# Spatial gating inside the key selection's stage, ties in four passes, setup and first norm as one stage, and a ratio with two pointer scalars

## The chip, the core and the metric

The kernel runs on one core of a Trainium2 chip. The metric is the device time of one execution in microseconds. TensorE (PE), VectorE (DVE), ScalarE (ACT), GpSimd (POOL) and the DMA queues of SyncE (SP) and ScalarE each work through a list of their own, and meet at semaphores.

## The reference

One sequence of 1024 tokens of width 1024 goes through two layers of a first kind and then two of a second kind. The parts that matter here:

```python
def rms_norm(x, g):
    y = xf * lax.rsqrt(jnp.mean(xf * xf, axis=-1, keepdims=True) + EPS)
    return (y * g.astype(jnp.float32)).astype(x.dtype)
...
def diff_attention(q, k, v, lam, rel_bias):
        ...
        a = p[0] - lam * p[1]
...
def spatial_gating_unit(u, v, g_v, b_v, w_s, b_s):
    vn = layer_norm(v, g_v, b_v).reshape(bn, s // CHUNK, CHUNK, A_GROUPS, A_GDIM)
    w_m = jnp.where(causal[None], w_s, jnp.zeros_like(w_s))
    mixed = jnp.einsum('gts,bcsgd->bctgd', w_m, vn) + b_s.T[:, :, None]
    return u * mixed.reshape(bn, s, A_WIDTH_2)
...
        score = jnp.where(causal[None], score, -jnp.inf)
        _, idx = lax.top_k(score, top)          # top = 256 keys for each query
...
    y_a = jax.nn.silu(z_a) * spatial_gating_unit(u, v, v_norm_g, v_norm_b, w_spatial, b_spatial)
```

Besides these the kernel needs tables at its start: the cosines and sines of the positions, the bias of each relative position (`onehot` times `rel_bias`), the silu of the condition, and the scalar `lam` of each first-kind layer.

## The kernel before

The program is a row of stages (`Phase`). Each stage gives every engine one list, and between two stages all engines meet at a barrier, so a stage lasts as long as its slowest engine, and nothing of the next stage starts before, its loads included. Activations lie in SBUF as 8 tiles of 128 tokens or 8 tiles of 128 features. For exactness a float32 matrix product is made as three products of rounded halves (`hh`, `hl` of the activations, `w_hi`, `w_lo` of the weights). `ps` is PSUM, 8 banks of 128x512.

**Start.** `setup_phase` makes the tables. PE multiplies `relb` by `onehot` into four banks, DVE copies them to `rows`, and SP stores these and waits for the store. Behind its copies DVE reduces the angles for the sine. `norm_phase` then loads `x` (8 tiles of 512 KB), ACT sums the squares of each tile, POOL takes the power -0.5 of four tiles at a time, DVE scales the four, PE transposes them into one of four banks (16 units, u = half of the tokens and feature tile), ACT applies the gain into `n_full`, and DVE makes `hh` by a copy and `hl` by a subtraction. ACT waits until `hl` of the unit two before is made. The first projection follows (`w_hi` by ACT, `w_lo` by DVE, products at L695).

**End of the selection.** In each second-kind layer `select_project_phase` makes the last four groups of 512 columns of the input projection: the queries, two gates, and `u`, over 32 chunks of weights. For each chunk ACT makes `w_hi`, POOL `w_lo` (L2248), PE 24 products. In the same stage the keys are selected: for query blocks 2 to 7 a binary search over 32 bits finds the score of the 256th key. DVE counts for blocks 7, 3, 4 and 2 (`BY_DVE`), ACT for 5 and 6 (`BY_ACT`). Blocks are of 128 queries on the partitions, block qb has (qb + 1) * 128 keys. POOL meanwhile turns the queries and applies the gates (`apply_gate`, two operations for each of 16 units, L2242 and L2244, counted by `gated`). When the cuts stand, DVE counts the keys above each cut (L2138) and settles ties in five passes for each block:

```python
equal = (scores == cut)                       # L2202
rank = running sum of equal                   # L2203, tensor_tensor_scan
rank = (rank <= left over) * equal            # L2204
rank = (scores > cut) + rank                  # L2205
scores = (rank - 1) * 1e30                    # L2206, the mask added to the scores later
```

`u` is the last group that PE makes; ACT empties its 8 banks into `u_t` (L2073). Then `spatial_phase`, a stage of its own, loads the weights of the gating and their bias, POOL zeroes the upper triangle (L2452), PE mixes the tokens of each chunk into 8 banks (L2481), DVE adds the bias from PSUM and multiplies by `0.5 * u_t` into one of three `s_tmp` (L2467, L2471), and POOL multiplies `y` by it (L2457). After it come the sparse attention heads (`heads_phase`, tag `x_`).

**The ratio.** In the differential heads of the first kind DVE divides two row sums and multiplies by `neg_lam` (L1234, L1236); POOL scales a row of probabilities by it.

## Time and profile before

| | us |
|---|---|
| median of 3 runs | 3238.22 |
| lowest and highest | 3235.09 to 3243.04 |
| the profiled execution, by the same clock | 3231.08 |
| its span in the trace | 3229.4 |

The profile is that of one execution; its span runs from the first to the last recorded instruction, and 1.7 us lie around it. A row of the timeline gives the start in us from the span's start, the duration, the engine, the line of the kernel, the operation, and in brackets how long the engine had idled and what ended that. "x8" merges eight instructions that follow one another. The clock column is the share of TensorE's full clock that was granted.

### The profile page before, as it was taken

How to read it: one execution, taken by the hardware profiler on the slowest of the kernel's cores; microseconds unless marked ns; L12 is line 12 of the kernel's file. 1: busy time of each engine (PE TensorE's matmuls, PEld its weight loads, DVE VectorE, ACT ScalarE, POOL GpSimd, SP SyncE). 2: the span in 40 equal slices, each digit the busy share in tenths (PEclk: the TensorE clock that was granted, in tenths of full speed). 3: DMA queues.
4: the chain of work that ended last, by engine and by line, in shares of the span. 5: the costliest groups of instructions: out<-in, count | busy, mean ns of one | idle time of the engine just before them, and what ended most of it. 6: DMA issues, size and time to landing. Idle time of an engine off the chain costs nothing. (4 is left out here: it accounts for less than half of the span.)

```text
span 3229.4 us, 40985 instructions
## 1 busy us (share of the span) xinstructions
PE 2743.8 (85%) x13680; PEld 2185.2 (68%) x13680; DVE 2103.4 (65%) x4302; ACT 1588.9 (49%) x3077; POOL 1126.8 (35%) x965
## 2 busy tenths in 40 slices
PE   5999788798979997888989798994889698994887
PEld 3877566677868775667877575773767575773766
DVE  4472388688434624868865358887767358887866
ACT  3221276588422114758863226572864326572861
POOL 0010177455001003765530003972631003982631
PEclk9999899899989997999999899997989899997999
DMA  3343210100324321000022100110022100110022
GB/s 107 108 143 100 88 38 7 40 1 12 132 67 144 122 69 53 26 17 23 1 105 79 52 21 23 46 37 23 1 112 78 59 20 23 47 37 23 1 86 79
DMA packets 90752, 181.93 MB, mean 56 GB/s; under 512 B 12552, under 2 KB 27912, under 8 KB 90504
## 3 DMA queue, kind: packets, MB, share of 16 engines
q1 hardware_dynamic: 74124, 150.69, 14.4%
q10 hardware_dynamic: 16416, 28.61, 3.0%
q8 instruction: 109, 1.79, 0.2%
q14 instruction: 103, 0.84, 0.1%
HBM read 149.87 MB, written 33.33 MB: 57 GB/s over the span
## 5 line engine op out<-in xcount | busy, mean ns | idle before, releaser
L695 PE MATMUL ps<-w_hi,hh 128*128 128x512 f32 (+1 forms) x640 | 243.1, 380 | 24.1 <-DVE w_lo L580 12.0
L1277 POOL TENSOR_SCALAR a_prob<-a_prob,a_ratio 128x1024 f32<-128x1024 f32 x64 | 72.0, 1125 | 508.5 <-DVE a_ratio L1236 505.9
L695 PE MATMUL ps<-w_lo,hh 128*128 128x512 f32 (+1 forms) x640 | 240.4, 376 | 0.0
L1699 PE MATMUL ps<-o_w_hi,hh 128*128 128x512 f32 x512 | 212.8, 416 | 32.5 <-DVE o_w_lo L1623 32.5
L695 PE MATMUL ps<-w_hi,hl 128*128 128x512 f32 (+1 forms) x640 | 239.3, 374 | 0.0
L2138 DVE TENSOR_SCALAR_CACHE_REDUCE select_rows<-masks,select_cuts 128x640 bf16<-128x640 f32 (+7 forms) x268 | 233.3, 874 | 0.2
L1699 PE MATMUL ps<-o_w_lo,hh 128*128 128x512 f32 x512 | 206.7, 404 | 0.0
L1699 PE MATMUL ps<-o_w_hi,hl 128*128 128x512 f32 x512 | 206.3, 403 | 0.0
L974 POOL TENSOR_SCALAR b_prob<-b_prob,b_recip 128x1024 f32<-128x1024 f32 x128 | 144.3, 1127 | 170.5 <-DVE b_recip L939 168.0
L1679 POOL TENSOR_TENSOR o_rstd<-o_rstd,nhalf 128x1 f32<-128x1 f32 x56 | 46.7, 833 | 420.3 <-DVE o_rstd L1560 240.6
L1225 DVE CUSTOM_DVE_ANT_0 a_prob<-ps,a_bias 128x1024 f32<-128x1024 f32 x128 | 151.4, 1220 | 53.0 <-PE ps L1362 51.4
L916 DVE TENSOR_TENSOR b_attn_t_lo<-ps,b_attn_t_hi 128x512 fp32r<-128x512 f32 x256 | 163.7, 679 | 16.3 <-ACT b_attn_t_hi L850 15.9
L932 DVE TENSOR_REDUCE b_neg_max<-ps 128x1 f32<-128x1024 f32 x128 | 156.2, 1220 | 19.6 <-PE ps L1043 19.2
L1180 ACT ACTIVATE a_prob<-a_prob,a_neg_max 128x1024 f32<-128x1024 f32 x128 | 146.3, 1150 | 34.3 <-DVE a_neg_max L1225 34.3
L2282 PE MATMUL ps<-hh,w_hi 128*128 128x512 f32 x384 | 152.1, 396 | 8.1 <-ACT y L2073 5.4
L871 ACT ACTIVATE b_prob<-ps,b_neg_max 128x1024 f32<-128x1024 f32 x128 | 143.4, 1120 | 30.7 <-DVE b_neg_max L932 30.0
L695 PEld LDWEIGHTS ps<-w_hi,hh 128*128 128x128 f32 x640 | 121.5, 190 | 52.8 <-DVE w_lo L580 20.9
L1975 PE MATMUL ps<-w_hi,hh 128*128 128x512 f32 (+1 forms) x384 | 140.0, 365 | 17.6 <-DVE w_lo L1943 12.6
L850 ACT ACTIVATE b_attn_t_hi<-ps 128x512 fp32r<-128x512 f32 x256 | 139.7, 599 | 31.0 <-PE ps L1009 30.5
L1280 POOL TENSOR_TENSOR a_prob<-a_prob 128x1024 f32<-128x1024 f32 x64 | 152.6, 2385 | 5.3
L1362 PE MATMUL ps<-a_rows 64*128 64x512 f32 x768 | 119.4, 448 | 39.4 <-DVE a_neg_max L1225 35.8
L2282 PE MATMUL ps<-hh,w_lo 128*128 128x512 f32 x384 | 151.6, 395 | 0.0
(350 smaller groups left out, 8216.3 us busy)
## 6 DMA issues: line engine op xcount, KB each, us to landing
w_early<-in_w_in SPq DMA_DIRECT2D x108, 256.0 KB, 2.8
ada_w<-in_w_ada ACTq DMA_DIRECT2D x96, 256.0 KB, 2.7
w_raw<-in_w_in SPq DMA_DIRECT2D x84, 256.0 KB, 2.7
xcur<-aq SPq DMA_DIRECT2D x16, 512.0 KB, 3.8
y<-xcur SPq DMA_DIRECT2D x16, 512.0 KB, 4.1
a_bias<-bias_tiles SPq DMA_DIRECT2D x8, 960.0 KB, 4.8
bq<-in_w_out SPq DMA_DIRECT2D x12, 512.0 KB, 4.1
closing_rows<-in_w_out SPq DMA_DIRECT2D x12, 512.0 KB, 4.5
```

The source lines that it names most:

```text
L695: mm = nc.tensor.matmul(o, lhs, rhs, start=(k == 0 and i == 0), stop=(k == K - 1 and i == 2))
L871: nc.scalar.activation(prob(g), src, ACT.Exp, bias=nm[:, g % NS:g % NS + 1], scale=sign, accum_out=sums[:, g % NS:g % NS + 1]).then_inc(ex ...
L916: nc.vector.tensor_tensor(atl[:, kk % SLOTS, lo:], ps[:, bank(e), lo:], ath[:, kk % SLOTS, lo:].bitcast(F32), ALU.subtract).then_inc(tl_do ...
L932: nc.vector.tensor_reduce(out, ps[:, pair:pair + 2, :].rearrange("p b n -> p (b n)"), AX, ALU.max, negate=True).then_inc(shifted, 1)
L974: nc.gpsimd.tensor_scalar(prob(b), prob(b), rr[:, b % NS:b % NS + 1], 0.5, ALU.mult, ALU.mult).then_inc(normed, 1)
L1180: nc.scalar.activation(row, row, ACT.Exp, bias=nm[:, g % NS, m:m + 1], scale=-1.0, accum_out=out).then_inc(exped, 1)
L1225: nc.vector.tensor_tensor_reduce(out=row, in0=ps[:, 2 * m:2 * m + 2, :].rearrange("p b n -> p (b n)"), in1=bias, scale=-1.0, scalar=3.0e38 ...
L1280: nc.gpsimd.tensor_tensor(row0(g), row0(g), row1(g), ALU.add).then_inc(combined, 1)
L1699: mm = nc.tensor.matmul(o, lhs, rhs, start=(k == 0 and i == 0), stop=(k == K - 1 and i == 2))
L1975: mm = nc.tensor.matmul(ps[:, b, 0:n], lhs, rhs, start=(k == 0 and i == 0), stop=(k == K - 1 and i == 2))
L2138: spare_free[z] = mark(nc.vector.tensor_scalar(spare[:, z, 0:(qb + 1) * P], values, against, None, op, ALU.add, accum_out=column(count_of, ...
L2282: mm = nc.tensor.matmul(ps[:, b, :], lhs, rhs, start=(k == 0 and i == 0), stop=(k == K - 1 and i == 2))
```

## The change

There are four parts.

1. `opening_phase` takes the place of `setup_phase` and `norm_phase`. The loads of `x` stand first on SP's queue, then `onehot`, the gains and the tables, then the first two weight chunks. The positions stand first on ACT's queue. PE transposes first and multiplies `onehot` afterwards, into banks 4 to 7; their copies to `rows` go from DVE to ACT, behind its gains. ACT writes `hh` directly, rounded on writing, and DVE makes `hl` in one operation from PSUM; the `n_full` step is gone, and a bank is free when `hl` is made.
2. `spatial_phase` is gone. Its loads, its mask, its products and its additions stand in `select_project_phase`: the loads go into the weight buffers (`w_early` and `w_raw`) once all `w_lo` are made, PE mixes behind its last projection, POOL multiplies `y` by `u_t` ahead of the bias (`weigh_gate`) and by the biased mixture after (`mix`), and DVE writes that mixture over `u_t` (`add_bias`), two units behind each of the last four tie blocks. `mask_weights` is the mask of L2452. The factor 0.5 is applied where ACT empties `u`.
3. The ties take four passes, with `rank` in the buffer of the gates' tanh (so DVE first waits for all gates, `gated` at 32). Blocks 5 and 6 are counted by ACT, by one more sign pass each; DVE counts its own four before the wait.
4. The ratio is a `tensor_scalar` with two pointer scalars.

```diff
+                for t in range(T):
+                    sp.dma_start(xt[:, t, :], x_from[t * P:(t + 1) * P, :]).then_inc(x_in[t], 16)
                 sp.dma_start(onehot[:, :], a["onehot"]).then_inc(bias_in, 16)
                 sp.dma_start(relb[:, :], a["rel_bias"]).then_inc(bias_in, 16)
+                sp.dma_start(env["g_cols"][:, :, :], a["pre_norm_g"]).then_inc(kept_in, 16)
...
                         kept_in, 16)
+                for ch, (tile, sem) in enumerate(early.slots):
+                    sp.dma_start(tile, early.weights(ch)).then_inc(sem, 16)
                 sp.wait_ge(copied, 4)
                 sp.dma_start(env["bias_rows"].ap(), rows[:, :]).then_inc(stored, 16)
                 sp.wait_ge(stored, 16)
...
+                for t in range(Q):
+                    square(t)
                 act.wait_ge(cond_in, 16)
                 nc.scalar.activation(cth[:, :], cin[:, :], ACT.Tanh, scale=0.5).then_inc(bent, 1)
+                for t in range(Q, T):
+                    square(t)
                 act.wait_ge(dotted, 1)
                 nc.scalar.activation(dots[:, :, :], dots[:, :, :], ACT.Exp).then_inc(exped, 1)
                 for e in range(2):
                     act.wait_ge(reduced, e + 1)
                     nc.scalar.activation(trig[:, e, :, :], red[:, e, :, :], ACT.Sin).then_inc(waved, 1)
+                act.wait_ge(kept_in, 96)
+                for u in range(2 * K):
+                    h, k = divmod(u, K)
+                    act.wait_ge(turned, u + 1)
+                    nc.scalar.activation(hh[:, k, h * BANK:(h + 1) * BANK], ps[:, u % 4, :], ACT.Identity,
+                                         scale=gain_cols[:, k:k + 1]).then_inc(gained, 1)
+                for n in range(4):
+                    act.wait_ge(mult, n + 1)
+                    nc.scalar.activation(rows[:, n * BANK:(n + 1) * BANK], ps[0:A_HEADS, 4 + n, :],
+                                         ACT.Copy).then_inc(copied, 1)
 
...
+                pe.wait_ge(made, 2)
+                for u in range(2 * K):
+                    h, k = divmod(u, K)
+                    pe.wait_ge(rows_ready, (h + 1) * Q)
+                    if u >= 4:
+                        pe.wait_ge(lo_done, u - 3)
+                    for j in range(Q):
+                        mm = nc.tensor.transpose(ps[:, u % 4, j * P:(j + 1) * P],
+                                                 xt[:, h * Q + j, k * P:(k + 1) * P], ident[:, :])
+                    mm.then_inc(turned, 1)
                 pe.wait_ge(bias_in, 32)
                 for n in range(4):
-                    nc.tensor.matmul(ps[0:A_HEADS, n, :], relb[:, :], onehot[:, n * BANK:(n + 1) * BANK],
+                    nc.tensor.matmul(ps[0:A_HEADS, 4 + n, :], relb[:, :], onehot[:, n * BANK:(n + 1) * BANK],
                                      start=True, stop=True).then_inc(mult, 1)
...
+                def split(u):
+                    h, k = divmod(u, K)
+                    dst = slice(h * BANK, (h + 1) * BANK)
+                    dve.wait_ge(gained, u + 1)
+                    nc.vector.scalar_tensor_tensor(hl[:, k, dst], ps[:, u % 4, :], gain_cols[:, k:k + 1],
+                                                   hh[:, k, dst].bitcast(F32), ALU.mult, ALU.subtract).then_inc(lo_done, 1)
...
+                scale_rows(0)
+                dve.wait_ge(bent, 1)
+                step(nc.vector.tensor_scalar(cth[:, :], cth[:, :], 1.0, 0.5, ALU.add, ALU.mult))
+                nc.vector.tensor_tensor(env["cond"][:, :], cin[:, :], cth[:, :], ALU.mult)
+                scale_rows(1)
+                for u in range(2 * K):
+                    split(u)
...
-                    nc.vector.scalar_tensor_tensor(r, s0[:, g % NS0:g % NS0 + 1], neg_lam, r, ALU.mult,
-                                                   ALU.mult).then_inc(ratio_done, 1)
+                    nc.vector.tensor_scalar(r, s0[:, g % NS0:g % NS0 + 1], neg_lam, r, ALU.mult,
+                                            ALU.mult).then_inc(ratio_done, 1)
...
+        rank_row = th[:, :, :].rearrange("p e n -> p (e n)")
+        wt = early.tile[:, :, :].rearrange("p e (g t) -> p (e g) t", t=P)
+        bs = w_raw[:, 0, :].rearrange("p (g t) -> p g t", t=P)
...
                             sp.dma_start(gb[:, e * BANK:(e + 1) * BANK], row(a[name][l])).then_inc(rows_in, 16)
+                sp.wait_ge(lo_done, C)
+                sp.dma_start(wt, a["w_spatial_2"][l]).then_inc(spatial_w_in, 16)
+                for e in range(2):
+                    src = a["b_spatial_2"][l].rearrange("(p e) t -> e p t", e=2)[e].unsqueeze(0).broadcast_to(
+                        [HD, K // 2, P])
+                    sp.dma_start(bs[e * HD:(e + 1) * HD, :, :], src).then_inc(spatial_b_in, 16)
...
-                        nc.scalar.activation(dst, ps[:, b, :], ACT.Copy).then_inc(emptied, 1)
+                        nc.scalar.activation(dst, ps[:, b, :], ACT.Copy, scale=0.5 if g == U else 1.0).then_inc(emptied, 1)
...
+                for j, qb in enumerate(BY_ACT):
+                    act.wait_ge(moved, 2 * (2 * BITS - 1) + j + 1)
+                    nc.scalar.activation(verdict[:, j:j + 1], negcut[:, j:j + 1], ACT.Identity,
+                                         bias=env["nhalf"][:, 0:1]).then_inc(judged, 1)
+                for j, qb in enumerate(BY_ACT):
+                    n = (qb + 1) * P
+                    act.wait_ge(judged, 2 * 2 * BITS + j + 1)
+                    nc.scalar.activation(spare[:, 2 + j, 0:n], scores(qb), ACT.Sign, bias=verdict[:, j:j + 1],
+                                         accum_out=signs[:, j:j + 1]).then_inc(above, 1)
                 empty(U)
...
+                def add_bias(z):
+                    p, h = units[z]
+                    if z == 0:
+                        dve.wait_ge(spatial_b_in, 32)
+                    dve.wait_ge(mixed, z + 1)
+                    dve.wait_ge(weighed, z + 1)
+                    nc.vector.tensor_tensor(half_of(u_t, p, h).rearrange("p (c t) -> p c t", t=P),
+                                            ps[:, z, :].rearrange("p (c t) -> p c t", t=P),
+                                            bs[:, p, :].unsqueeze(1).broadcast_to([P, 4, P]), ALU.add).then_inc(biased, 1)
...
-                dve.wait_ge(moved, 4 * BITS)
-                last = mark(nc.vector.tensor_scalar(cut[:, 4:6], negcut[:, :], -1.0, None, ALU.mult))
-                after(last)
-                for qb in ORDER:
+                for qb in BY_DVE:
                     last = count(qb, column(cut, qb), scores(qb), ALU.is_gt)
                 after(last)
-                after(mark(nc.vector.tensor_scalar(count_of[:, :], count_of[:, :], -1.0, float(TOPK), ALU.mult, ALU.add)))
-                for qb in ORDER:
+                mark(nc.vector.tensor_scalar(count_of[:, 0:4], count_of[:, 0:4], -1.0, float(TOPK), ALU.mult, ALU.add))
+                last = mark(nc.vector.tensor_scalar(minus[:, 0:4], cut[:, 0:4], -1.0, None, ALU.mult))
+                after(last)
+                dve.wait_ge(gated, 4 * T)
+                for i, qb in enumerate(ORDER):
                     n = (qb + 1) * P
-                    equal, rank = work[:, 0, 0:n], work[:, 1, 0:n]
+                    equal, negative = work[:, 0, 0:n], column(minus, qb)
+                    rank = rank_row[:, 0:n]
+                    if qb in BY_ACT:
+                        j = BY_ACT.index(qb)
+                        negative = negcut[:, j:j + 1]
+                        dve.wait_ge(moved, 4 * BITS)
+                        dve.wait_ge(above, j + 1)
+                        mark(nc.vector.tensor_scalar(column(cut, qb), negative, -1.0, None, ALU.mult))
+                        after(mark(nc.vector.tensor_scalar(column(count_of, qb), signs[:, j:j + 1], -0.5, TOPK - 0.5 * n,
+                                                           ALU.mult, ALU.add)))
                     after(mark(nc.vector.tensor_scalar(equal, scores(qb), column(cut, qb), None, ALU.is_equal)))
                     after(mark(nc.vector.tensor_tensor_scan(rank, equal, equal, 0.0, ALU.add, ALU.bypass)))
-                    after(mark(nc.vector.scalar_tensor_tensor(rank, rank, column(count_of, qb), equal, ALU.is_le, ALU.mult)))
-                    after(mark(nc.vector.scalar_tensor_tensor(rank, scores(qb), column(cut, qb), rank, ALU.is_gt, ALU.add)))
-                    after(mark(nc.vector.tensor_scalar(scores(qb), rank, 1.0, -MASKED, ALU.subtract, ALU.mult)))
+                    after(mark(nc.vector.scalar_tensor_tensor(rank, rank, column(count_of, qb), scores(qb), ALU.is_gt,
+                                                              ALU.subtract)))
+                    mark(nc.vector.tensor_scalar(scores(qb), rank, negative, MASKED, ALU.is_gt, ALU.mult))
+                    if i >= 2:
+                        add_bias(2 * i - 4)
+                        add_bias(2 * i - 3)
...
+                    pool.wait_ge(emptied, 8 * U + z + 1)
+                    nc.gpsimd.tensor_tensor(half_of(y, p, h), half_of(y, p, h), half_of(u_t, p, h),
+                                            ALU.mult).then_inc(weighed, 1)
+
+                def mix(z):
+                    p, h = units[z]
+                    pool.wait_ge(biased, z + 1)
+                    nc.gpsimd.tensor_tensor(half_of(y, p, h), half_of(y, p, h), half_of(u_t, p, h),
+                                            ALU.mult).then_inc(y_done, 1)
 
                 for ch in range(C):
...
+                mask_weights()
+                pool.wait_ge(gated, 4 * T)
+                for z in range(8):
+                    weigh_gate(z)
+                for z in range(8):
+                    mix(z)
...
+                pe.wait_ge(masked, 1)
+                pe.wait_ge(v_ready, T)
+                for z, (p, h) in enumerate(units):
+                    pe.wait_ge(emptied, 8 * U + z + 1)
...
+                            mm = nc.tensor.matmul(ps[e * HD:(e + 1) * HD, z, c_ * P:(c_ + 1) * P],
+                                                  v[:, 4 * h + c_, feats], wt[:, 2 * p + e, :], start=True, stop=True)
+                    mm.then_inc(mixed, 1)
```

The removed functions are printed above, and `scale_rows` and `square` do what their loops in `norm_phase` did. The order in which the engines issue their work shows two places. ScalarE at the program's start, before the change (`n_sq` is the squares of `x`, `trig` the sines, the branches are the ends and starts of stages):

```order
L272 ACTIVATE c_tanh<-c_in 128x8
L274 ACTIVATE lam_dots<-lam_dots 128x4
L277 ACT_TABLE_LOAD
L277 ACTIVATE trig<-reduced 128x256 x2
L86 UNCONDITIONAL_BRANCH
L359 UNCONDITIONAL_BRANCH
L365 ACTIVATE n_sq,n_ss<-n_x 128x1024 x8
L372 ACTIVATE n_full<-ps,g_cols 128x512 x16
L86 UNCONDITIONAL_BRANCH
```

and after it:

```order
L284 ACTIVATE n_sq,n_ss<-n_x 128x1024 x4
L299 ACTIVATE c_tanh<-c_in 128x8
L284 ACTIVATE n_sq,n_ss<-n_x 128x1024 x4
L303 ACTIVATE lam_dots<-lam_dots 128x4
L306 ACT_TABLE_LOAD
L306 ACTIVATE trig<-reduced 128x256 x2
L311 ACTIVATE hh<-ps,g_cols 128x512 x16
L315 ACTIVATE rows<-ps 4x512 x4
L86 UNCONDITIONAL_BRANCH
```

The squares now stand ahead of the tanh and the sines, the 16 gains write `hh`, and the four copies of `rows` close the stage.

VectorE from the last count of the selection to the second tie block, before (the scan prints as SCALAR_TENSOR_TENSOR):

```order
L2198 TENSOR_SCALAR select_counts<-select_counts 128x6
L2202 TENSOR_SCALAR select_rows<-masks,select_cuts 128x1024
L2203 SCALAR_TENSOR_TENSOR select_rows<-select_rows 128x1024
L2204 SCALAR_TENSOR_TENSOR select_rows<-select_rows,select_counts 128x1024
L2205 SCALAR_TENSOR_TENSOR select_rows<-masks,select_cuts,select_rows 128x1024
L2206 TENSOR_SCALAR masks<-select_rows 128x1024
L2202 TENSOR_SCALAR select_rows<-masks,select_cuts 128x512
```

and after the change, the third and the fourth tie block, and the start of the fifth:

```order
L2234 TENSOR_SCALAR select_rows<-masks,select_cuts 128x640
L2235 SCALAR_TENSOR_TENSOR p_tanh<-select_rows 128x640
L2236 SCALAR_TENSOR_TENSOR p_tanh<-p_tanh,select_counts,masks 128x640
L2238 TENSOR_SCALAR masks<-p_tanh,select_minus 128x640
L2185 TENSOR_TENSOR u_t<-ps,w_raw 128x512 x2
L2234 TENSOR_SCALAR select_rows<-masks,select_cuts 128x384
L2235 SCALAR_TENSOR_TENSOR p_tanh<-select_rows 128x384
L2236 SCALAR_TENSOR_TENSOR p_tanh<-p_tanh,select_counts,masks 128x384
L2238 TENSOR_SCALAR masks<-p_tanh,select_minus 128x384
L2185 TENSOR_TENSOR u_t<-ps,w_raw 128x512 x2
L2231 TENSOR_SCALAR select_cuts<-select_negcuts 128x1
L2232 TENSOR_SCALAR select_counts<-select_signs 128x1
```

A block has four passes, `rank` lies in `p_tanh`, the additions of the bias (`u_t<-ps,w_raw`) come in pairs behind a block, and the two small operations at a block of ACT's turn its sums into a count.

## Rows read from the trace of the kernel before

**Rows 1.** The page, busy time of each engine over the span.

```profile
PE 2743.8 (85%) x13680; PEld 2185.2 (68%) x13680; DVE 2103.4 (65%) x4302; ACT 1588.9 (49%) x3077; POOL 1126.8 (35%) x965
```

**Rows 2.** Stretches: length, busy time of each engine, clock, DMA share, GB/s.

```profile
0.00:21.67 21.67, 6.98 (x8) 0.82 (x8) 10.03 (x30) 3.81 (x6) 1.00 (x9) 1.00 0.28 58
...
21.67:58.37 36.70, 13.01 (x65) 10.08 (x65) 23.12 (x44) 21.34 (x34) 2.04 (x2) 0.89 0.33 129
...
2171.82:2207.29 35.47, 11.09 (x48) 8.67 (x46) 34.34 (x44) 4.79 (x8) 1.02 (x1) 0.72 0.00 0
...
2207.29:2232.35 25.06, 9.08 (x128) 8.84 (x128) 14.20 (x16) 0.00 (x0) 11.23 (x9) 0.70 0.11 32
```

**Rows 3.** Timeline of the start: start us, us, engine, line, operation, [idle before].

```profile
4.65 6.98 PE L283 MATMUL ps<-onehot,relb 32*4 32x512 f32 x8 [4.65 <-DMA relb<-in_rel_bias]
...
12.37 0.33 SPq L246 DMA_DIRECT2D bias_rows<-rows  x1
...
13.67 1.28 ACT L277 ACT_TABLE_LOAD   x1
...
21.67 3.85 SPq L348 DMA_DIRECT2D n_x<-in_x  x8
...
25.30 1.06 ACT L365 ACTIVATE n_sq<-n_x 128x1024 f32<-128x1024 f32 x1 [5.78 <-DMA n_x<-in_x]
...
31.63 2.74 DVE L384 TENSOR_SCALAR n_x<-n_x,n_rstd 128x1024 f32<-128x1024 f32 x4 [1.14 <-POOL n_rstd L356]
...
55.51 0.42 DVE L390 CAST hh<-n_full 128x512 fp32r<-128x512 f32 x1
...
58.37 0.79 PE L695 MATMUL ps<-w_hi,hh 128*128 128x512 f32 x1 [6.69 <-DVE w_lo L580]
```

**Rows 4.** Two stretches of 1 us within the transposes, columns as in the second group.

```profile
44.00:45.00 1.00, 0.84 (x5) 0.47 (x4) 0.97 (x3) 0.62 (x2) 0.00 (x0) 0.50 0.00 0
...
48.00:49.00 1.00, 0.56 (x5) 0.36 (x5) 0.97 (x3) 0.69 (x1) 0.00 (x0) 1.00 0.00 0
```

**Rows 5.** One line: a split of a PSUM bank; ns min/median/max.

```profile
L1203 DVE SCALAR_TENSOR_TENSOR a_rows<-ps,a_rows x32: 673/690/693, 370.5 to 1368.1; 128x512 fp32r<-128x512 f32 x32
```

**Rows 6.** VectorE's timeline at the end of the selection and in the gating.

```profile
2162.93 0.33 DVE L2163 TENSOR_SCALAR select_cuts<-select_kept,select_cuts 128x1 f32<-128x1 f32 x2
...
2171.82 1.04 DVE L2193 TENSOR_SCALAR select_cuts<-select_negcuts 128x2 f32<-128x2 f32 x1 [8.55 <-ACT select_negcuts L2097]
...
2178.43 0.75 DVE L2202 TENSOR_SCALAR select_rows<-masks,select_cuts 128x1024 f32<-128x1024 f32 x1
...
2206.66 0.63 DVE L2206 TENSOR_SCALAR masks<-select_rows 128x896 f32<-128x896 f32 x1
...
2222.19 1.26 DVE L2471 SCALAR_TENSOR_TENSOR s_tmp<-s_tmp,u_t 128x512 f32<-128x512 f32 x1
```

**Rows 7.** GpSimd's and ScalarE's timelines in the same stretch.

```profile
2170.29 1.29 POOL L2244 TENSOR_TENSOR y<-y,p_tanh 128x512 f32<-128x512 f32 x1
...
2213.08 1.10 POOL L2452 TENSOR_SCALAR_AFFINE_SELECT s_wt<-s_wt 128x1024 f32<-128x1024 f32 x1 [40.24 <-DMA s_wt<-in_w_spatial]
...
2231.09 1.26 POOL L2457 TENSOR_TENSOR y<-y,s_tmp 128x512 f32<-128x512 f32 x1 [0.63 <-DVE s_tmp L2471]
...
2178.12 5.42 ACT L2073 ACTIVATE u_t<-ps 128x512 f32<-128x512 f32 x8 [6.40 <-PE ps L2282]
```

**Rows 8.** Groups by line on VectorE: busy us, mean ns.

```profile
L2205 DVE SCALAR_TENSOR_TENSOR select_rows<-masks,select_cuts,select_rows 128x1024 f32<-128x1024 f32 (+5 forms) x12 | 11.4, 952 | 0.4
```

**Rows 9.** VectorE's timeline beside a busy GpSimd, and that stretch.

```profile
1994.67 2.01 DVE L2148 TENSOR_TENSOR masks<-masks,select_rows 128x768 int32<-128x768 int32 x1
...
1997.38 1.09 DVE L2148 TENSOR_TENSOR masks<-masks,select_rows 128x896 int32<-128x896 int32 x1
...
1994.07:2009.23 15.16, 13.31 (x50) 10.74 (x51) 14.77 (x13) 10.30 (x29) 14.24 (x9) 0.82 0.39 104
```

**Rows 10.** One line: the ratio of the differential heads.

```profile
L1236 DVE SCALAR_TENSOR_TENSOR a_ratio<-a_sums,neg_lam,a_ratio x64: 218/220/1859, 385.4 to 1413.0; 128x1 f32<-128x1 f32 x64
```

227 lines of the change are left out of this document (68 added, 159 removed).

## The prediction

> **What bounds the kernel now.** I read the page first. TensorE is busy 85% of the span [rows 1], but that is an average, and a change inside one stage is worth what that stage's slowest engine gives. So I cut the trace at the barriers around the change [rows 2]. There TensorE is nearly idle. In the first stage it works 7.0 us of 21.7, in the next 13.0 of 36.7. From the moment the cuts stand in a second-kind layer (2171.8) to the last tie (2207.3) it works 11.1 of 35.5, VectorE 34.3. In the gating stage it works 9.1 of 25.1, VectorE 14.2 and GpSimd 11.2. These stretches are chains on VectorE and GpSimd that nothing covers. The second such layer lies 728 us later and I take it as the same, since it runs the same lists. The stretches come to 58.4 + 2 x 60.5 us, and the change touches all of them.
>
> **The start, now 58.4 us to the first projection product** [rows 3]. Today SP issues the loads of `x` at 21.7, behind the tables, and ACT squares the first tile at 25.3. Now they are issued at about 0.8. The first tile then lands at some 4.5 (3.6 after its issue, as today), ACT has issued its own loads and loaded its table (1.28) by 5.5. Four squares take until 30.3 today (the scaling at 31.63 less the 1.14 for the power and 0.17 for the variance), so 1.26 each. Eight, the tanh, and up to 1 us for table loads that share the queues (28% busy over the first 21.7 us, [rows 2]) end at 17.0. ACT then has the exponential, one more table load of 1.28 and two sines: gains can begin at 19.4. VectorE's table work of 7.3 us (its 10.0 busy in [rows 2] less four copies of 0.68) lies below the squares. Its second half waits for the squares: 17.0 + 0.17 + 1.14 + 2.74 = 21.1, and there the splits begin.
>
> Each split is one operation from PSUM, 0.69 [rows 5], or 0.61 to 0.66 from start to start; today a copy (0.42) and a subtraction (0.69) make 1.06 from start to start, and the last pair begins at 55.5 [rows 3]. Sixteen take 10.6: to 31.7, and VectorE's last table steps 1.3 more, 33.0. But a new tail is longer. TensorE gets its last transposes when split 12 of 16 is done (29.0), ends them at 29.8, and only then multiplies `onehot`. That took 6.98 us [rows 3] behind an idle engine, which I take for the low level of the clock. Inside the transposes of today the granted clock stands at the low level in one microsecond and at full in another [rows 4], so it is 3.5 or 7.0. Then come ACT's last copy (0.7), the store's issue (0.33, [rows 3]) and its landing. How long the store takes does not show; 3.6 is the first load's time to its use, and I take 2.2, with 1.5 to 3.6 as bounds. The stage ends between 36.5 and 40.5, I take 38.2. From VectorE's last subtraction to the first product today it is 1.7 (58.37 less 56.65, the end of the pair that began at 55.51). So the first product stands at about 39.9 where it stood at 58.4: **18.5 us less**, from 16.2 to 20.3 by these bounds. `w_early` is in by then. Moving the `rows` copies off VectorE costs nothing more than this tail, since ACT has nothing behind its gains.
>
> **The selection's tail, twice.** Today VectorE ends the search at 2163.3, waits 8.55 us for ACT's cuts, and has counted all blocks at 2178.4 [rows 6]. Now it counts its own four in that gap (3.3 us) and waits for the last gate, which GpSimd ends at 2171.6 [rows 7]. So ties begin at 2171.65: 6.8 less. ACT's two added sign passes (2.3 us) end at 2174.3; it next empties `u` at 2178.1 [rows 7], so they lie in its idle time, and without that cover they would delay TensorE's mixing by 2.3 only, which isn't late.
>
> Five passes over six blocks took 2178.4 to 2207.3, 28.9. The dropped one is 11.4 / 2 = 5.7 per layer [rows 8] and its gaps 0.2: 23.0 remain. Two pairs of small operations at ACT's blocks add 0.6, eight additions of the bias from PSUM 8 x 0.66 = 5.3. Alone, VectorE would end at 2171.65 + 28.9 = 2200.6.
>
> It isn't alone. GpSimd masks at about 2177 (the load waits for the last `w_lo` at 2172.8; from the load to the mask it was 4.2), multiplies from 2178.8 as the banks are emptied, and mixes behind the additions: 1.1 + 8 x 1.29 + 6 x 1.27 = 19.0 us of work before the last pair. Rows of today show what that costs. A 768-wide operation of VectorE with two SBUF inputs took 2.01 us, a 896-wide one 1.09 [rows 9]. Over that stretch of 15.16 GpSimd is busy 14.24; VectorE's twelve passes there would take 9.3 at the rate of the 1.09, so it loses 5.9 us to 12 or so of GpSimd's work, 0.5 per us. In the gating stage an operation of 0.69 takes 1.26 beside a GpSimd one [rows 6], 0.45 per us. The additions read PSUM and keep their time, so some 3 of the 19 us fall where they harm nothing. I take 0.58 per us, a little above both rows because the tie passes leave no gaps: 16 x 0.58 = 9.3, ties end at 2209.9. The last two mixes end 1.9 later, 2211.8. TensorE mixes at 2183 to 2192 (9.1 of work, [rows 2]) and isn't waited for.
>
> The stage and the gating together ended at 2232.35 [rows 7]: 20.6 less in each layer, **41 for both**. What becomes late next is GpSimd's last pair.
>
> The Trainium skill (GPSIMD Engine Reference, Key points) says that GpSimd shares its SBUF interfaces with VectorE and contends with operations in a two-port mode or with two SBUF inputs, which is what a tie block consists of; the rows above agree. It speaks against this part, and gives no price. A sum by it with every microsecond of GpSimd's work added to VectorE's (a loss of 1) is the second rival; with the rows' loss it is the sum above.
>
> **The ratio.** 64 operations of 0.22 us [rows 10]. The new form shows nowhere with two pointers; the nearest rows with one pointer are the search's steps at 0.15 to 0.2, so it gains at most 64 x 0.05 = 3 us, loses no more, and most lies beside other work. I take 0.
>
> **Sum.** 18.5 + 41 = 59.5 off the profiled execution's 3231.1 is 3171.6. The median of the runs is 7 us above that execution; off 3238.2 it is **3179**, the number I give, since what is measured is a median.
>
> **The rivals.**
>
> *Light contention.* GpSimd's work hardly slows the ties, as it doesn't slow the search's counts. Ties end at 2200.6, the stage at 2202.6: 29.8 per layer, and with the start's 18.5 some 78, so 3160. For it: some passes may use one input only. Against: both rows of [rows 9]. 10%.
>
> *Full serialisation.* Each microsecond of GpSimd is lost to VectorE: ties end at 2200.6 + 16, the stage at 2218.5, 13.8 per layer: 46 in all, 3192. For it: GpSimd's eight multiplies stand back to back, as in no stretch of the gating. 15%.
>
> *The start gives half.* The loads of `x` share the queues with small pieces: over the first 21.7 us they are 28% busy with little data (58 GB/s), so 6.1 us of queue time. If all of it came first, squares, splits and the store all stand up to 6 us later, at the low clock and with the slow store 8: 10 in place of 18.5, 3187. 10%.
>
> *Slower.* GpSimd as the new bound: 16 operations from 2178.8. They decide from the point where they end past 2232.4, that is from 3.35 us each; alone they take 1.29 [rows 7]. At 4 us each the stage would end at 2243 and the kernel, both layers counted, 2 us slower, the start's gain included. Nothing in the rows comes near. 1%.
>
> *The change does nothing.* It would need the gain to be given back at a later DMA wait, of 60 us. The loads of the next stages are issued inside them, so they move along. 2%.
>
> The forecast has 62%. The range takes in light contention to full serialisation: 3160 to 3197, the upper end also for a store and clock at their slow bounds with it. A measurement of this kernel tells 0.3%, about 10 us, from no change. All cases but the last two lie 40 us and more below, so faster has 0.97, same 0.02, slower 0.01.
>
> **What the profile of the changed kernel would show.** The first projection product at 38 to 42 us; splits at a spacing of 0.61 to 0.7 from about 21; the `onehot` products behind the transposes, with VectorE idle at the stage's end. The first tie pass 0.1 us behind the last gate, some 8.3 us behind the search's last step. Tie passes of 128x1024 and of 128x512 at today's times before GpSimd's multiplies begin and longer under them, additions of the bias still 0.68. From the last gate to the barrier some 40 us, 61 today. It is wrong if that stretch is nearer 31 or 47, or if the transposes begin past 20 us, which would mean that the loads of `x` came late.

## The result

The changed kernel takes 3182.94 us, the median of 4 runs (3181.74 to 3185.18), the kernel before 3239.69 (3235.09 to 3243.04, 4 runs). The ratio is 0.9826, 95% interval 0.9813 to 0.984: faster by 52 to 61 us. The forecast was 3179, with a range of 3160 to 3197.

The page and three stretches of the changed kernel, columns as in [rows 1] and [rows 2]:

```profile
PE 2747.1 (86%) x13680; PEld 2191.3 (69%) x13680; DVE 2070.8 (65%) x4254; ACT 1594.8 (50%) x3093; POOL 1154.7 (36%) x981
...
0.00:20.00 20.00, 0.34 (x2) 0.36 (x3) 9.17 (x26) 11.18 (x20) 2.08 (x11) 1.00 0.90 258
...
2155.92:2198.69 42.77, 18.44 (x177) 15.80 (x175) 40.00 (x36) 7.21 (x15) 26.93 (x18) 0.77 0.07 19
2163.18:2176.93 13.75, 11.18 (x146) 9.91 (x144) 13.54 (x11) 4.08 (x7) 13.75 (x9) 1.00 0.01 1
```

The second stretch runs from the last gate to the barrier and takes 42.77 us, where it was 2232.35 - 2171.58 = 60.77 [rows 7]. VectorE is busy in 40.0 of it: it is still the chain. The third is GpSimd's eight first multiplies. Both engines are full there, and more than half of the loss turned out to lie there (6.7 of 11.0 us, run 6).

The timeline of the start, columns as in [rows 3]:

```profile
0.79 4.04 SPq L244 DMA_DIRECT2D n_x<-in_x  x8
...
5.07 1.06 ACT L284 ACTIVATE n_sq<-n_x 128x1024 f32<-128x1024 f32 x1
...
8.21 11.02 SPq L251 DMA_DIRECT2D b_ada_cols<-in_b_ada_cols  x1
...
18.23 1.06 ACT L284 ACTIVATE n_sq<-n_x 128x1024 f32<-128x1024 f32 x1 [0.91 <-DMA n_x<-in_x]
...
23.45 2.42 ACT L311 ACTIVATE hh<-ps,g_cols 128x512 fp32r<-128x512 f32 x4 [1.94 <-DMA qk_gain<-in_k_norm_g]
24.18 11.26 DVE L353 SCALAR_TENSOR_TENSOR hl<-ps,g_cols,hh 128x512 fp32r<-128x512 f32 x16 [0.42 <-ACT hh L311]
...
33.51 3.59 PE L332 MATMUL ps<-onehot,relb 32*4 32x512 f32 x8
...
37.75 0.32 SPq L259 DMA_DIRECT2D bias_rows<-rows  x1
...
41.95 0.79 PE L681 MATMUL ps<-w_hi,hh 128*128 128x512 f32 x1 [4.86 <-DVE w_lo L566]
```

The first product stands at 41.95 us where it stood at 58.37 [rows 3]. Read from the top: the loads of `x` are issued at once, but the squares of tiles 2 to 8 each wait 0.4 to 0.9 us for their load and end at 19.3 in place of the forecast 17.0. The splits begin at 24.2 (forecast 21.1), and the stage ends with the chain named in the prediction: last transposes, `onehot` products, a copy, a store.

The selection's end in the first such layer, VectorE's ties and GpSimd's part:

```profile
2156.02 1.70 DVE L2234 TENSOR_SCALAR select_rows<-masks,select_cuts 128x1024 f32<-128x1024 f32 x1 [4.01 <-POOL y L2279]
...
2163.30 2.26 DVE L2235 TENSOR_TENSOR_SCAN p_tanh<-select_rows 128x512 f32<-128x512 f32 x1
...
2168.55 1.56 DVE L2234 TENSOR_SCALAR select_rows<-masks,select_cuts 128x640 f32<-128x640 f32 x1
2170.14 2.44 DVE L2235 TENSOR_TENSOR_SCAN p_tanh<-select_rows 128x640 f32<-128x640 f32 x1
...
2190.66 2.96 DVE L2235 TENSOR_TENSOR_SCAN p_tanh<-select_rows 128x896 f32<-128x896 f32 x1
...
2195.45 1.28 DVE L2185 TENSOR_TENSOR u_t<-ps,w_raw 128x512 f32<-128x512 f32 x2
```

```profile
2163.18 13.75 POOL L2289 TENSOR_TENSOR y<-y,u_t 128x512 f32<-128x512 f32 x8 [0.86 <-ACT u_t L2077]
...
2196.21 2.48 POOL L2295 TENSOR_TENSOR y<-y,u_t 128x512 f32<-128x512 f32 x2 [4.47 <-DVE u_t L2185]
```

The first tie follows the last gate by 0.1 us, as forecast. The scan of 512 columns takes 2.26 us beside GpSimd, the additions from PSUM keep their 0.64 each. One sign of the prediction failed: the first pass, of 1024 columns, was to keep its 0.75 us and takes 1.70, beside GpSimd's last `w_lo` (2155.87 to 2157.17).

### The profile page after: what moved, and what is told of

Same layout as the page of the kernel before. It is cut to its first block and busy times, and to the rows that moved or that the text cites. A ratio compares the mean times of both kernels' runs of the same rounds, so it can differ in the third digit from the quotient of the medians.

```text
span 3183.4 us, 40934 instructions
## 1 busy us (share of the span) xinstructions
PE 2747.1 (86%) x13680; PEld 2191.3 (69%) x13680; DVE 2070.8 (65%) x4254; ACT 1594.8 (50%) x3093; POOL 1154.7 (36%) x981
## 5 line engine op out<-in xcount | busy, mean ns | idle before, releaser
L2151 DVE TENSOR_SCALAR_CACHE_REDUCE select_rows<-masks,select_cuts 128x1024 bf16<-128x1024 int16 (+7 forms) x264 | 229.7, 873 | 0.2
L918 DVE TENSOR_REDUCE b_neg_max<-ps 128x1 f32<-128x1024 f32 x128 | 156.2, 1221 | 20.1 <-PE ps L1029 19.7
L502 ACT ACTIVATE w_hi<-w_raw 128x512 fp32r<-128x512 f32 (+1 forms) x56 | 33.7, 601 | 239.4 <-PE ps L681 229.7
```

Source lines behind the costliest of these rows:

```text
L918: nc.vector.tensor_reduce(out, ps[:, pair:pair + 2, :].rearrange("p b n -> p (b n)"), AX, ALU.max, negate=True).then_inc(shifted, 1)
L2151: spare_free[z] = mark(nc.vector.tensor_scalar(spare[:, z, 0:(qb + 1) * P], values, against, None, op, ALU.add, accum_out=column(count_of, ...
```

## The experiments

All times below are medians; the ratio stands against runs of the kernel before on the same chip, taken beside them. Before took 3234.18 us beside runs 1 to 4, 3229.87 beside runs 5 to 7 (one execution each), 3237.83 beside runs 8 to 11 and 3236.09 beside run 12. The code shown with a run is shortened to what matters.

**1. The opening alone.** The kernel before with the change's `opening_phase` only.

```diff
+opening_phase(... x_from, gain_cols, hh, hl ...)   # as changed
 select_project_phase, spatial_phase, the ratio       # as before
```

> The kernel before with the opening stage alone (selection, ties, gating and ratio as before). If the parts are independent, the gain is what stands between the two traces at the first projection product, 58.37 against 41.95: 16.4 us, so 3223, and that product at 42. The rival, that the opening's gain is partly given back at a later wait (the two traces differ by 46 us at the end where 16.4 + 2 x 18 = 52.4 were gained in the changed stages), gives 10 us, 3230.

3221.68 us, ratio 0.9955 (0.9939 to 0.9971): 14.6 us less, 9 to 20 by the interval. The first product stands at 41.53, so the stage alone gives the 16.8 us of the trace. Whether later stages give some of it back isn't told: the interval holds both the 16.4 and the rival's 10.

**2. The selection's stage alone**, with the opening and the ratio of before.

```diff
+select_project_phase   # as changed, gating inside
-spatial_phase
 opening_phase, the ratio   # as before
```

> The kernel before with the selection, the ties and the gating of the change (opening and ratio as before). Independent parts: 60.8 us from the last gate to the barrier become 42.8 in each layer, 36 us less, 3204. The rival, that the stages behind give some of it back because TensorE has idled since 2182 and comes cold (6 us missing between the traces), gives 30, 3210.

3206.16 us, ratio 0.9897 (0.9872 to 0.9922), 25 to 41 us less: its runs scatter (3196.61 to 3212.53), so it doesn't tell the two apart. The traces say a little more: the heads' stage behind the selection takes 157.1 and 158.2 us here, 157.5 and 155.9 in the kernel before, so that stage gave back 1.9 of the 6 in this pair. With the first run the two parts sum to 48 us; the whole gave 52 to 61. The parts add up within what the runs tell.

**3. Five passes in place of four**, all else as changed.

```diff
-rank = (rank > count) - scores;  scores = (rank > -cut) * MASKED
+rank = (rank <= count) * equal;  rank = (scores > cut) + rank
+scores = (rank - 1) * -MASKED
```

> The changed kernel with five passes for each tie block, as before, all else as changed. If GpSimd's work costs VectorE a fixed sum (so many us lost for each us of its work), the fifth pass adds what it costs alone, 5.7 + 0.2 in each layer: 12 us, 3195. The rival, that passes are stretched by a factor all through (40.7 us where 28.9 would do, 1.4), gives 8.3 in each layer, 16.6 us, 3199.5. In the trace: from the last gate to the barrier 48.7 or 51.1.

3191.77 us, ratio 0.9863 (0.9847 to 0.9879), some 12 us above the changed kernel (0.0037 of 3238). The stage's end is where ScalarE begins the next one:

```profile
2204.22 1.06 ACT L820 ACTIVATE x_stage<-kv 128x1024 fp32r<-128x1024 f32 x1 [37.52 <-PEq L86]
```

In the changed kernel that row stands at 2199.02; from the first tie it is 49.35 us here and 43.00 there. The dropped pass was worth some 6.3 us a layer, near its own length (5.7, [rows 8]) and not the rival's 8.3: GpSimd's work is a fixed amount, and with it the loss, so one more pass stretches into the time when GpSimd is idle.

**4. The bias by TensorE.** A product with one row of weights puts the bias into PSUM ahead of each of the 64 value products; VectorE's addition becomes the multiplication by the gate, and GpSimd's mixes go.

```diff
+matmul(o, ones[1 row], brow[p], start=True, stop=False)
-matmul(o, v, wt, start=True, stop=True)
+matmul(o, v, wt, start=False, stop=True)
-u_t = ps + bs        (VectorE);  y = y * u_t   (GpSimd)
+y = ps * y           (VectorE)
```

> The changed kernel with the bias of the gating added by TensorE (one product of a row of ones and the bias ahead of each product), so that VectorE multiplies PSUM by y into y in place of adding the bias, and GpSimd's eight second multiplies fall away. The contention theory: six of them lie beside the tie passes and cost 6 x 1.29 x 0.6 = 4.6, the last two end 2.0 behind VectorE: 6.6 us less in each layer, 13 in all, 3170. If only the tail counts (the contention comes from the first eight alone), 4 in all, 3179. The added products take TensorE some 14 us in each layer where it idles; if they come too late for the multiplies, VectorE waits and the gain is gone.

3273.96 us, ratio 1.0118 (1.0101 to 1.0134), slower than before. VectorE's timeline, and TensorE's:

```profile
2196.32 0.69 DVE L2182 TENSOR_TENSOR y<-ps,y 128x512 f32<-128x512 f32 x1 [6.74 <-PE ps L2346]
```

```profile
2181.41 0.68 PE L2345 MATMUL ps<-w_raw,ones 1*64 1x128 f32 x2
2182.02 0.69 PE L2346 MATMUL ps<-w_early,v 128*64 128x128 f32 x2
...
2180.00:2190.00 10.00, 10.00 (x34) 4.58 (x32) 3.02 (x5) 0.00 (x0) 0.00 (x0) 0.50 0.00 0
```

Each product, of either kind, takes 0.62 us from start to start, and a unit 9.87. VectorE waits for seven of the eight units: TensorE needs 75.7 us for all (2169.93 to 2245.6), where the expectation had 14 for the added products. The clock stands at its low level, 0.50, in this stretch; ahead of it, at 1.00, a product takes 0.36 (2170 to 2174). The low clock alone isn't it, as run 8 shows.

**5. GpSimd idle behind the mask.** `y` leaves out both multiplications of the gating.

```diff
-dve.wait_ge(weighed, z + 1)       # in add_bias
-for z in range(8): weigh_gate(z)
-for z in range(8): mix(z)
```

> The changed kernel without GpSimd's sixteen multiplies of the gating in each second-kind layer, so y there is the gate alone; GpSimd still masks the weights. If GpSimd's work is all that stretches the ties, VectorE needs what it needs alone: 28.9 us from the last gate to its last addition, plus 0.7 beside the last w_lo and 0.6 beside the mask, so 30 where it took 40.8, and the barrier comes 2.0 earlier still. The rival, that the new forms of the passes (pointer scalars, rank in another buffer) are slower by themselves, leaves 35 or more.

One execution, 3158.01 us. Ties begin at 2155.92 and the last addition ends at 2185.67: 29.75 us.

```profile
2155.92 1.70 DVE L2233 TENSOR_SCALAR select_rows<-masks,select_cuts 128x1024 f32<-128x1024 f32 x1 [4.02 <-POOL y L2278]
...
2161.97 1.32 DVE L2233 TENSOR_SCALAR select_rows<-masks,select_cuts 128x512 f32<-128x512 f32 x1
2163.33 1.23 DVE L2234 TENSOR_TENSOR_SCAN p_tanh<-select_rows 128x512 f32<-128x512 f32 x1
...
2165.78 0.55 DVE L2233 TENSOR_SCALAR select_rows<-masks,select_cuts 128x640 f32<-128x640 f32 x1
2166.36 1.49 DVE L2234 TENSOR_TENSOR_SCAN p_tanh<-select_rows 128x640 f32<-128x640 f32 x1
...
2180.54 2.02 DVE L2234 TENSOR_TENSOR_SCAN p_tanh<-select_rows 128x896 f32<-128x896 f32 x1
```

Every pass that lay beside a multiplication is back at its own time: 1.23 for 2.26, 0.55 for 1.56, 1.49 for 2.44, 2.02 for 2.96. The first pass (1.70) still lies beside the last `w_lo`, and one of 512 columns (1.32) beside the mask. So the multiplications cost 40.8 - 29.75 = 11.0 us per layer, and the last mixes add 2.0 behind. The rival, new forms that are slower by themselves (35 or more), fell.

**6. Mixes without weighs.** The gating leaves out the factor `u`; the eight mixes stay.

```diff
-dve.wait_ge(weighed, z + 1)       # in add_bias
-for z in range(8): weigh_gate(z)
```

> The changed kernel without GpSimd's first eight multiplies (y times u), so the gating leaves out u. Ten us of work less beside the ties. At a loss of 0.65 per us VectorE ends 6.7 earlier, 34 us from the last gate to its last addition; if work on both sides is serialised (loss 1), 10 earlier, 30.5.

One execution, 3170.26 us. The ties begin at 2158.53 and the last addition ends at 2192.59, 34.06 us. So the six mixes beside the ties cost VectorE 4.3 us and the eight weighs the other 6.7. At the 1.27 and 1.29 us that one takes alone [rows 7] that is 0.56 and 0.65 us per us of GpSimd's work, or 0.7 and 0.8 us for each multiplication. A loss of 1 per us (30.5) fell.

**7. The loads of `x` with less beside them.** ScalarE's small loads go to SP's queue behind the eight loads of `x`.

```diff
 sp.dma_start(xt[t], x[t])   # x8
+sp.dma_start(cin, ...); sp.dma_start(lam_in, ...); sp.dma_start(consts, ...); sp.dma_start(g_in, ...)
-act.dma_start(cin, ...)   # and the other three
-scale_rows(0)    # VectorE: behind the lambda steps
+scale_rows(0)    # VectorE: ahead of them
```

> The changed kernel with ACT's queue issuing only the two loads for the angles at the start; the condition, lam, constants and g_sub loads go to SP's queue behind x, and VectorE does the lam steps behind the first scaling. The eight squares run from 5.07 to 19.4 now, 1.8 a piece. If the loads on ACT's queue slow those of x, the pace goes back to the 1.26 of before, the squares end at 15, and all stands some 3 us earlier (the first projection product at 39). The rival, that the queues are slow in the first microseconds whatever is issued, or that x is slowed by what stands behind it on its own queue, leaves the squares' end at 19 and the product at 42.

One execution, 3185.71 us, first product at 42.02: nothing gained.

```profile
10.19 1.06 ACT L291 ACTIVATE n_sq<-n_x 128x1024 f32<-128x1024 f32 x1
...
15.83 0.21 ACT L299 ACTIVATE c_tanh<-c_in 128x8 f32<-128x8 f32 x1 [4.49 <-DMA c_in<-in_c]
```

The fourth square ends at 11.3 where it ended at 11.8; then ScalarE waits 4.49 us for `c_in`, which now stands behind `x`. From there on the squares find their tiles landed and end at 20.1. The edit brought its own wait, so it doesn't tell how much the small loads cost `x`; that stays open.

**8. The bias by TensorE in one batch.** Sixteen bias products of 512 columns ahead of all 64 value products; the rest as in run 4.

```diff
+for e in range(2):
+    for z in range(8): matmul(ps[e, z, :], ones[1 row], brow[p] x4, start=True, stop=False)
 for z in range(8): for c_, e: matmul(ps[...], v, wt, start=False, ...)
```

> The changed kernel with the spatial bias put into PSUM by TensorE, in 16 products of 512 columns and one row of weights that all stand ahead of the 64 value products, so that the two kinds do not alternate; VectorE then multiplies PSUM by the gate in place of adding the bias, and GpSimd's eight mixes go. If alternation was what made the earlier form cost 9.9 us a unit, the last add ends where it did in the run whose GpSimd work stopped after the mixes' place, with the eight weighs alone charged: 34 us from the first tie becomes about 36.5 (29.75 plus 0.6 of 11 to 14 us of weighs less what they no longer meet), and the 2.0 us of the last mix go: 4 to 6.5 us per layer, 3170 to 3175 us in all. If the cost sits in the value products themselves once a group of accumulation is open, the units still take over 5 us each and the kernel is slower than the changed one, 3210 us or more.

3198.95 us, ratio 0.988 (0.9866 to 0.9893): by the ratios 77 us faster than run 4, 17 slower than the changed kernel. TensorE's groups here (busy us, mean ns), and three stretches:

```profile
L2343 PE MATMUL ps<-w_raw,ones 1*64 1x512 f32 x32 | 19.7, 906 | 0.0
L2351 PE MATMUL ps<-w_early,v 128*64 128x128 f32 x128 | 9.8, 331 | 0.0
...
2166.80:2169.00 2.20, 2.20 (x7) 0.71 (x7) 2.18 (x2) 0.60 (x1) 2.20 (x2) 1.00 0.00 0
...
2172.00:2186.00 14.00, 14.00 (x21) 3.56 (x19) 3.27 (x3) 0.00 (x0) 4.46 (x3) 0.50 0.00 1
...
2186.40:2190.00 3.60, 3.60 (x35) 3.60 (x36) 0.69 (x1) 0.00 (x0) 0.00 (x0) 0.50 0.00 0
```

A product has two records. In the last row, with the clock at 0.50, 35 records take 3.60 us, 0.10 each; in run 4, at the same 0.50, 34 take 10.0, 0.29 each. So a value product took 0.62 us when one-row products stood between, and 0.21 in a row of its kind: alternation cost it 0.4 us. The Trainium skill (TensorEngine Tiling (Array Packing), Key Properties) says that a change of the tiling mode drains TensorE. The trace agrees that the change is what costs; that one row of weights is such a mode, no run here shows. My second expectation there, over 5 us a unit in the value products, fell (1.2). But the first did too, since it had no time for the bias products: sixteen of 512 columns take 19.7 us, during which the clock falls from 1.00 to 0.50 (at the pace of the first stretch, 7 records in 2.20 us, they would take 10, an estimate), and VectorE waits for them:

```profile
2188.42 0.69 DVE L2182 TENSOR_TENSOR y<-ps,y 128x512 f32<-128x512 f32 x1 [13.08 <-PE ps L2351]
```

**9. The bias rows early.** The four `onehot` products go between transposes, the copies between gains, and the gains wait for `g_cols` alone.

```diff
 for u in range(16): transposes(u)
+    if u in (4, 6, 8, 10): onehot product (u - 4) / 2
 for u in range(16): gain(u)
+    if u in (6, 8, 10, 12): copy of row (u - 6) / 2
```

> The changed kernel with the four bias rows' products and copies interleaved with the middle of the opening's transposes instead of standing behind them, and with the norm's gain columns waited for by themselves. The theory that the opening ends with the chain of last transposes, 3.6 us of products, a copy and a store of 2.3 us behind them expects the stage to end with VectorE's tables at about 37 us in place of 40.2, the first product of the next stage at about 38.7 in place of 41.95, and 3.2 us less, 3180. The rival, that the copies placed inside the loop slow a ScalarE that is as busy there as VectorE (0.69 us against 0.70 per unit), gives back up to 4 x 0.59 = 2.4 us of it, 3182.

3188.18 us, ratio 0.985 (0.9836 to 0.9864): 5 us slower than the changed kernel by the medians, 8 by the ratios, against both expectations. TensorE's groups in 24 to 44 us, here and then in the changed kernel:

```profile
L330 PE MATMUL ps<-ident,n_x 128*128 128x128 f32 x48 | 10.7, 403 | 1.3 <-DVE hl L359 1.3
L338 PE MATMUL ps<-onehot,relb 32*4 32x512 f32 x8 | 7.5, 1034 | 0.0
```

```profile
L327 PE MATMUL ps<-ident,n_x 128*128 128x128 f32 x48 | 8.2, 325 | 2.0 <-DVE hl L353 1.9
L332 PE MATMUL ps<-onehot,relb 32*4 32x512 f32 x8 | 3.6, 587 | 0.0
```

The same records take longer: 403 ns against 325, 1034 against 587. That is TensorE's low clock. Duration of one transpose (ns, min/median/max) in the kernel before, at a granted clock of 0.50 and of 1.00 [rows 4], then here, then in the changed kernel:

```profile
L403 PE MATMUL ps<-ident,n_x x12: 336/418/448, 43.7 to 46.8; 128*128 128x128 f32 x12
L403 PE MATMUL ps<-ident,n_x x9: 272/273/301, 47.9 to 50.0; 128*128 128x128 f32 x9
```

```profile
L330 PE MATMUL ps<-ident,n_x x8: 421/421/475, 38.4 to 40.0; 128*128 128x128 f32 x8
L330 PE MATMUL ps<-ident,n_x x7: 272/273/273, 41.3 to 41.9; 128*128 128x128 f32 x7
```

```profile
L327 PE MATMUL ps<-ident,n_x x9: 421/421/421, 26.4 to 28.1; 128*128 128x128 f32 x9
L327 PE MATMUL ps<-ident,n_x x14: 272/273/300, 28.8 to 31.0; 128*128 128x128 f32 x14
```

The clock rose at 41 us here, after a stretch in which a `onehot` product stood behind every eight transposes, and at 28 us in the changed kernel, after transposes alone. Run 11, with the same order, shows 41.7. How the small products hold it down isn't shown. The clock column doesn't show this. It reads 1.00 wherever the trace has no clock entry, and the first entries stand at 41.2 and 28.5 us; the 1.00 in the first stretch of [rows 2] is no measurement either.

TensorE is busy without a gap from 26 to 42 us, gains and splits wait for its transposes, the last split ends at 44.3 in place of 35.4, and the next stage's first product stands at 47.2. The bound moved to TensorE, which neither of my theories had named.

**10. The ratio's old instruction** in the changed kernel.

```diff
-tensor_scalar(r, s0, neg_lam, r, mult, mult)
+scalar_tensor_tensor(r, s0, neg_lam, r, mult, mult)
```

> The changed kernel with the ratio's instruction of before (218 to 220 ns each in the trace of before, against 273 ns for the form with two pointer scalars). The theory that VectorE is not what ends these stages expects no change against the changed kernel, 3183 us plus or minus 3. The rival, that 64 instructions longer by 53 ns lie on the path in part, expects 1.5 to 3.5 us less, 3180 or under.

3182.91 us, ratio 0.9827 (0.9813 to 0.9841): no difference, though an interval of 4.5 us to each side can't exclude the rival's 1.5 to 3.5. The traces do: from the first product to the end of the span it is 3141.3 us here and 3141.5 in the changed kernel. The instruction itself differs, changed kernel first, then this one:

```profile
L1222 DVE TENSOR_SCALAR a_ratio<-a_sums,neg_lam,a_ratio x64: 271/273/276, 369.6 to 1395.0; 128x1 f32<-128x1 f32 x64
```

```profile
L1222 DVE SCALAR_TENSOR_TENSOR a_ratio<-a_sums,neg_lam,a_ratio x64: 219/220/1875, 367.3 to 1398.1; 128x1 f32<-128x1 f32 x64
```

The new form is 53 ns longer, 3.4 us of VectorE over 64 of them, and none of it shows.

**11. Runs 8, 9 and 10 together.**

> The batched bias, the early bias rows and the ratio's old instruction together in the changed kernel. If each gives what it is expected to give alone (8 to 13 us, 3.2 us, 0 us), 3167 to 3172 us.

3202.71 us, ratio 0.9892 (0.9878 to 0.9905), some 21 us above the changed kernel. The losses of 8 (17) and 9 (8) add up nearly; nothing new.

**12. The gating's multiplications by VectorE.** GpSimd does none; VectorE weighs, adds and mixes between the ties.

```diff
-for z in range(8): weigh_gate(z)   # GpSimd
-for z in range(8): mix(z)          # GpSimd
+for work in (weigh, add_bias, mix): work(2 * i - 4); work(2 * i - 3)   # VectorE
```

> The changed kernel with the eight weighs and eight mixes of the spatial gate done by VectorE, between the ties, in place of GpSimd; GpSimd is idle behind the mask. VectorE's part without any multiply took 29.75 us from first tie to last add; 16 multiplies of 128x512 from SBUF at 0.62 to 0.66 us (half of the 1.23 to 1.29 that two of them or one of 1024 columns take in the traces) add 10.1 to 10.6, so the last one ends 40.1 us behind the first tie, and nothing follows it. The theory that GpSimd's multiplies cost VectorE 0.56 to 0.65 us per us (13.75 + 6 x 2.7 us of them, 11.0 us lost, and 2.0 us of tail) expects the stage to end 2.4 us sooner per layer than with GpSimd, 3178 us in all. The rival, that the loss is not contention but a wait for GpSimd's results that the ties absorb, expects VectorE to lose with each multiply that it takes over, and the stage to end no sooner, 3183 to 3190.

3174.9 us (3172.08 to 3177.68, 5 runs), ratio 0.981 (0.9785 to 0.9834): 8 us less than the changed kernel by the medians, 5 by the ratios, and the two intervals overlap. The times alone don't settle it; the trace does. VectorE's first tie and last mix, and the next stage's first row:

```profile
2158.68 1.70 DVE L2243 TENSOR_SCALAR select_rows<-masks,select_cuts 128x1024 f32<-128x1024 f32 x1 [4.01 <-POOL y L2289]
...
2196.83 1.29 DVE L2185 TENSOR_TENSOR y<-y,u_t 128x512 f32<-128x512 f32 x2
...
2198.41 1.06 ACT L820 ACTIVATE x_stage<-kv 128x1024 fp32r<-128x1024 f32 x1 [27.90 <-PEq L86]
```

From first tie to last mix it is 39.4 us (expected 40.1), and from first tie to the next stage 39.7, where the changed kernel takes 43.0: 3.3 us a layer. Doing one multiplication costs VectorE 0.6 us (39.4 - 29.75 for sixteen); one that GpSimd did beside it cost 0.8 (11.0 for fourteen). So VectorE gains 1.3 us, and the tail of 2.0 goes. The rival, that VectorE loses with each one it takes over, fell.

## Why the prediction held

**The selection's tail: right in its steps, short in the loss beside GpSimd.** Ties start at the last gate (0.1 behind it). ScalarE's added passes and TensorE's mixing were covered. From the last gate to the barrier it took 42.8 us where 40.2 was forecast. Of the 2.6, run 5 puts 0.85 in what is left without the multiplications (29.75, forecast 28.9), and 1.7 in the loss beside them (11.0, forecast 9.3). The 29.75 isn't VectorE alone, though. In it the first pass lies beside the last `w_lo` (1.70 for 0.75) and another beside the mask (1.32 for 0.48), 1.8 us together. Without these VectorE's own work is 28.0, 0.9 below the forecast, and GpSimd's work beside it cost 12.8 in all, where the sum had 9.3. The price per us was close, 0.58 against 0.56 and 0.65. But I had left the last `w_lo` out, and 3 of 19 us as harmless beside the additions. With 8 x 1.29 + 6 x 1.27 = 17.9 us of multiplications, at 11.0, 0.61 per us holds for the whole of it. So the term was mis-sized by its discount and by the missing `w_lo`, and the error in VectorE's own work hid part of it. It came to 18.2 us per layer in place of 20.6: ScalarE's stage from its first `w_hi` to the next stage's first row is 238.8 and 239.0 us before, 220.6 and 220.7 after.

Both rivals on this were tested. Light contention (3160) needed the ties at their own times, and they have them only without GpSimd's work. Full serialisation would have lost 16 us. The Trainium skill (GPSIMD Engine Reference, Key points) names operations with two SBUF inputs and those in a two-port mode as the ones that contend. The trace agrees for the passes with two SBUF inputs, and the additions with an input in PSUM lost nothing (0.64 beside GpSimd and without it). The comparison has one input and was hit hardest in proportion (0.55 to 1.56); whether it runs in such a mode, no run here shows. In microseconds all passes beside the eight weighs lost about the same, 0.8 to 1.0 each, whatever their kind.

**The opening: right in kind, 16.4 for 18.5, inside its bounds.** The step that fell short is the squares' pace. I took 1.26 us each from a stage in which `x` had been the main load. Now they came 1.88 apart, each waiting for its tile, and ended at 19.3 for 17.0. The splits began at 24.2 for 21.1: 2.3 of these 3.1 us are the squares, 0.3 the small steps up to the scaling, and 0.4 the gains' wait for the last small load. That load was issued at 19.75, behind an issue that held SP for 11.0 us. ScalarE idled 1.94 for it, but most of that lay beside the second scaling, which ended at 23.75. The splits then took 11.26 for 10.6, because TensorE's clock was low until 28 us (run 9) and the gains waited for its transposes. One guess about the end went the other way: the `onehot` products ran at full clock, 3.59 us for 6.98 before, where the sum had about 5.2. The store took 2.5 us at most, near the 2.2 given. So the rival in which the start gives half named the right weakness, slow loads of `x`, at 2.3 us in place of up to 6.

Over nine executions of this same opening, the first product stood between 39.86 and 42.63, the earliest in run 10. There the gains began at 21.89, all but the first 16 of the 64 transposes ran at full clock, and the splits took 10.62 in place of 11.26:

```profile
21.89 10.33 ACT L311 ACTIVATE hh<-ps,g_cols 128x512 fp32r<-128x512 f32 x16 [1.53 <-DMA qk_gain<-in_k_norm_g]
22.73 10.62 DVE L353 SCALAR_TENSOR_TENSOR hl<-ps,g_cols,hh 128x512 fp32r<-128x512 f32 x16
...
L327 PE MATMUL ps<-ident,n_x x48: 272/273/303, 23.6 to 31.2; 128*128 128x128 f32 x48
```

So 39.9 was the good end of what this stage does, and when the clock rises (22.8 us in run 10, 31.0 in the latest of the nine) is part of it. What slows the loads of `x` was tried once (run 7) and stays open.

**The ratio: 0, right** (run 10), though its reason was half wrong: the new form was taken as slightly faster and is slower, and its 3.4 us of VectorE show nowhere in the time.

**The sum.** The changed stages give 16.4 + 36.4 = 52.8 us by the traces, where 59.5 was forecast. The two spans differ by 46.0 only. Of the rest, 3.5 lies in the closing stage between the two second-kind layers, which took 139.99 us in the trace of before and 143.46 in that of after; fourteen traces of it, none changed there, lie between 140.0 and 143.5. Another 2.2 lies in the last heads' stage (155.9 and 158.2; 155.8 to 159.5 over the fourteen). A single pair of executions doesn't tell more. The medians tell 52 to 61 us. That the forecast came within 4 us is luck in part: it was 7 us too optimistic on the stages, and the ratio of the medians came out 4 us above what the stages show.

## What to carry to other kernels

Before work goes to GpSimd beside a VectorE chain, price what VectorE loses. Where VectorE would take 0.6 us for an operation that GpSimd takes 1.3 for, and loses 0.6 of each us, that is 0.8, handing it over loses time, and a tail is added. A pass that is dropped from such a chain gives its own length and no more. When a stage is started early, its loads meet others that had been spread out: take their pace as a range, not from the old place. Small products set between the steps of a chain on TensorE can cost far more than at its end; look there at the pace of the records, since the clock column can stand at 1.00 for want of entries.

## What the runs showed of the hardware

- Beside GpSimd's multiplications, VectorE's comparison with one SBUF input went from 0.55 to 1.56 us (640 columns), a scan of 512 from 1.23 to 2.26, and each pass beside the eight weighs lost 0.8 to 1.0. Operations with an input in PSUM kept their time. GpSimd's own slowed from 1.29 to 1.72 on average (13.75 / 8).
- Alternating products of one row and of 128 rows took 0.62 us each at a granted clock of 0.50 (1.2 GHz) and 0.36 at 1.00; not alternated, those of 128 rows took 0.21 at the same clock. A one-row product of 128 columns by itself was not run.
- The granted clock fell from 1.00 (2.4 GHz) to 0.50 during one-row products, though TensorE shows as busy all the time (run 8: 1.00 in 2166.8 to 2169.0, 0.50 in 2172 to 2186). With a 32-row product behind every eight transposes it rose at 41.2 us, with transposes alone at 28.5 (run 9 and the changed kernel; first clock entry of each trace).
- `tensor_scalar` with two pointer scalars takes 273 ns on a 128x1, `scalar_tensor_tensor` 220.
